# Output projection and first up chains computed in two parts of the tokens, with split weights kept, and the last conditioning columns moved into the up stage

## The chip, the cores and the metric
The kernel runs on one core of one Trainium2 chip. The metric is the device time of one execution in microseconds. Three executions took 1133.63, 1133.76 and 1136.33 us; their median is 1133.76 us. TensorE does the matrix products (PE in the profile), ScalarE (ACT), VectorE (DVE) and GpSimd (POOL) the rest, and SyncE (SP) issues the DMA copies.

## The reference
One inference step of one decoder layer, for a prompt of 512 tokens and 8 samples of one token each, model width 1024. The samples have their own conditioning vectors. What matters here is the part behind the mixing stage:

```python
mix = (jax.nn.sigmoid(z_pool) * y_pool + jax.nn.sigmoid(z_att) * y_att) @ w_out   # 1024 x 1024
x = x + gate_m * rms_norm(mix, g_post_mix)
h = modulate(rms_norm(x, g_pre_ffn), shift_f, scale_f)
hu_ext = jnp.concatenate([conv_hist, h @ w_up], axis=1)                            # 1024 x 5632
hc = b_conv
for j in range(CONV_W):                                                            # width 3, causal
    hc = hc + hu_ext[:, j:j + T] * w_conv[j]
a, b = jnp.split(hc, 2, axis=-1)
ffn = (jax.nn.gelu(a, approximate=True) * b) @ w_down                              # 2816 x 1024
x = x + gate_f * rms_norm(ffn, g_post_ffn)
```

The vectors shift, scale and gate come from silu(c) @ w_ada + b_ada, six times 1024 columns. The prompt and the samples go through the same weights. The updated key and value caches of the samples are outputs as well: almost all of their rows are copies of the inputs, shifted by one.

## The kernel before, in words
Activations lie transposed: channels on the 128 partitions, the 520 tokens (512 of the prompt and 8 samples) along the free dimension, eight tiles of 128 channels. All large products are made in three terms, high part of weights by high part of activations, high by low, low by high, each with fp32r operands. A unit is a block of weights, 128 output channels by 1024 input channels (512 KB). For each of the eight tiles of a unit and each of the three terms, TensorE issues two products, one for each half of 260 tokens (`blocks`, L1289): 48 products a unit. The sums go to two accumulators in turn, `acc[0]` and `acc[1]`; the engine that evacuates one counts `acc_free` up, and `take` waits for it.

A unit is loaded by SP into one of four raw buffers (`unit`, L333), which waits until the unit four before has been split (`lo_ready`). ACT writes the high part (`split`, L651), DVE the low part (L892). There are two places for split weights; a place is reused when TensorE is done with the unit in it (`unit_done`). The split of unit n + 2 stands behind unit n in ACT's and DVE's order. Every engine works its own list of instructions in order, SP too; the lists are written out by hand and meet at semaphores.

The units in order are 60 of the combined projection, 14 of the mixing stage, 8 of the output projection (`out`), 44 of the up projection (22 pairs (i, 0) and (i, 1), the a and the b half), and 24 of the down projection.

Output projection: for each of its units ACT copies the sum to `mixT` (L817) and writes its square to `sq` (L820), DVE adds that to `ssq` (L1212). Two more pieces lie between these units on TensorE. The conditioning vectors are made from w_ada in 24 steps of 256 columns: SP loads 1 MB (`ada_load`, L345), TensorE multiplies it (`ada`, L1333, 16 instructions), DVE evacuates, TensorE folds the parts (`fold`, L1343), DVE adds the bias (`modulation`). The last four steps (`OADA` to `OADA + 3`) give gate_f, which only the last norm uses. They have two buffers, `ada_last`; the load of step s waits until step s - 2 has been multiplied. TensorE issues them behind output units 4 to 7. In SP's list two of the loads come behind the load of output unit 3 and two behind that of unit 7. The old convolution inputs of the samples are transposed before the output projection (L1640), while TensorE waits for the merged activations.

Then the two norms, all tokens at once. Post norm: sum over partitions (`sum_columns`, L1355), reciprocal root on ACT and DVE (`inverse_root`, `root`), spread over the partitions (`spread`, L1361), and for each of eight tiles two DVE operations that update x (L1231, L1233). ACT squares the new x (L826), POOL adds the eight squares one after another (`sum_tiles`, L590), and sum, root and spread come again. Then DVE multiplies (L1250), ACT modulates (L680) and writes the high part (L683), DVE the low part (L964); the first up unit takes its tiles as they come.

Up chain i, two units: ACT evacuates a sum twice, into `he` (L842) and, times the last tap plus the bias, into `cv` (L843). DVE adds the two other taps, ACT takes the Gelu of the a half, DVE multiplies, ACT writes the high and DVE the low part of the result.

Beside each up unit SP issues one pair of cache copies (`copy`, L356); three pairs of such copies lie between output loads 0 to 2 and three between 3 to 5.

Of the kernel before, what the change touches and what calls it, by code (L numbers as in the profile page):

```python
# [12 lines left out]
P = 128  # L13
# [55 lines left out]

SUMS = (  # L70
    [("pair", p, k) for p in range(PAIRS) for k in range(NU)] + [("map", i) for i in range(8)] + [("pp", i) for i in range(8)]
    + [("pa", i) for i in range(8)] + [("out", i) for i in range(8)] + [("up", i, h) for i in range(FT) for h in range(2)]
# [6 lines left out]
PLACE = [0, 1, 2] + [n % 2 for n in range(1, len(UNITS) - 2)]  # L79
LAST = {n: max(i for i in range(n) if PLACE[i] == PLACE[n]) for n in range(3, len(UNITS))}  # L80
# [10 lines left out]
def program(nc, ins, outs):  # L91
# [5 lines left out]
    with ExitStack() as ctx:  # L97
# [42 lines left out]
        norm_u = put("norm_u", [KT, TC], F32, r_z)  # L140
# [19 lines left out]
        ada_raw += [put(f"ada_last{i}", [KT, 2 * P], F32, r_z + FULL + AW * i) for i in range(2)]  # L160

        def ada_slot(s):
            return ada_raw[s if s < SADA else 2 if s == SADA else 8 + s % 2 if s < OADA else 10 + s % 2]
# [3 lines left out]
        w_lo.append(put("w_lo2", [UW], F32R, r_more + UW * 4))  # L167
        S = new("S", [2, 2, 256])
# [51 lines left out]
        g_hi, g_lo = put("g_hi", [FT, TC], F32R, r_ff), put("g_lo", [FT, TC], F32R, r_ff + FT * TC * 4)  # L220
        r_cv = r_ff + 2 * FT * TC * 4
        cv = [[put(f"cv{a}{b}", [TC], F32, r_cv + (2 * a + b) * 2080) for b in range(2)] for a in range(2)]
        gm = [put(f"gm{b}", [TC], F32, r_cv + (4 + b) * 2080) for b in range(2)]
# [6 lines left out]
        conv_rows = put("conv_rows", [2 * NB, P], F32, r_ada)  # L230
        cst = put("cst", [2, NB * 2 * FT], F32, r_ada + 8192)
# [13 lines left out]
        psR = acc[1][:, 0, 400:405]  # L245
        accv = [a[:, :, 0:HALF] for a in acc]
        roots = {1: psT, 2: psS, 3: psS, 4: psS}

        def rs_p(n):
            return roots[n][:, 0:TP]  # L250

        def rs_s(n):
            return roots[n][:, TP:TP + NB] if n == 1 else roots[n][:, TP + P - NB:TP + P]

        def halves(x):
            return x.rearrange("p (a b) -> p a b", a=2)

# [50 lines left out]
        conv_used, conv_turned, ssqd = sem("conv_used"), sem("conv_turned"), sem("ssqd")  # L308
# [11 lines left out]
        def steps_to(t):  # L320

            return t // STEPS * (STEPS + 2) + t % STEPS

# [4 lines left out]
        def _(sp):  # L328
# [178 lines left out]
            sp.wait_ge(pv_done, 1)  # L507
            sp.dma_start(conv_rows[0:2 * FT, :, :], ins["state_conv"][0].rearrange("b j (m c) -> m (b j) c", c=P)).then_inc(conv_loaded, 16)
# [12 lines left out]
            ada_load(OADA + 3)  # L521

            for i in range(FT):
                for h in range(2):
                    unit(("up", i, h), block_of(w_up, i * P + h * FF))
                    copy(2, 2 * i + h + 36)

# [29 lines left out]
        def _(pool):  # L557
# [25 lines left out]
            def sum_tiles(base, first):  # L583
                for k in range(KT):
                    pool.wait_ge(squared, first + k + 1)
                    if k == 0:
                        pool.tensor_copy(ssq[:, :], sq[:, 0, :]).then_inc(ssqd, 1)
                    else:
                        pool.wait_ge(ssqd, base + k)
                        pool.tensor_tensor(ssq[:, :], ssq[:, :], sq[:, k % 2, :], ALU.add).then_inc(ssqd, 1)  # L590
# [41 lines left out]
            sum_tiles(8, 0)  # L632

            pool.wait_ge(tail_stored, 32)
            for i in range(FT):
                for half in range(2):
                    evacuated(pool, ("up", i, half))
# [1098 lines left out]
```

## Time and profile before
| | |
|---|---|
| median of three executions | 1133.76 us |
| the profiled execution | 1135.69 us, of which the span of the trace is 1133.8 us |
| TensorE products | busy 1059.3 us, 93% of the span |
| VectorE, ScalarE, GpSimd | busy 485.5, 417.8 and 119.7 us |
| mean granted TensorE clock | 0.955 of full speed |
| data moved by DMA | 216.01 MB, mean 191 GB/s |

The times of a trace are microseconds from the start of the span. Busy time of TensorE counts a product from issue to its modelled end, so that a busy row does not say that it works at its peak; the distance between starts says that. The span is 1.9 us shorter than the execution around it.

### The profile page before, as it was taken

The page shows a single profiled execution, that of the slowest core. Times are in us where ns is not written, and L with a number is a line of the kernel's source. Part 1 is how long each engine was busy: PE and PEld are TensorE (multiplying, and loading weights), DVE is VectorE, ACT ScalarE, POOL GpSimd, SP SyncE. Part 2 cuts the span into 40 slices and gives each one's busy share as a digit, 9 for nine tenths or more (in the row PEclk, how much of TensorE's full clock was granted, in tenths as well). Part 3 has the DMA queues.
Part 4 walks back from the last instruction along what each step waited for, and adds up shares of the span by engine and source line. Part 5 has one row for each costly group of instructions (what it writes and reads, how often), then busy time and mean ns, then how long its engine had stood idle before and what let it go on. Part 6 is the DMA issues. An engine that isn't in the chain of part 4 may idle for free.

```text
span 1133.8 us, 20595 instructions
## 1 busy us (share of the span) xinstructions
PE 1059.3 (93%) x8653; PEld 991.8 (87%) x8653; DVE 485.5 (43%) x884; ACT 417.8 (37%) x667; POOL 119.7 (11%) x165
## 2 busy tenths in 40 slices
PE   5999999999999999979898795599999999999996
PEld 3899999999999999868748794599999999999994
DVE  5533233322432244254814335656565655522224
ACT  5424423332443234244202233544444544422222
POOL 1000300040004001405402202200000000000000
PEclk8899999999999999979999897699999999999996
DMA  9885767567656774243926537066666666555312
GB/s 324 247 277 199 224 223 250 186 216 244 236 186 212 244 243 131 77 139 120 309 98 199 184 111 252 27 198 225 223 224 222 219 220 210 156 172 162 117 36 75
DMA packets 226856, 216.01 MB, mean 191 GB/s; under 512 B 6173, under 2 KB 191901, under 8 KB 226749
## 3 DMA queue, kind: packets, MB, share of 16 engines
q1 hardware_dynamic: 226765, 214.70, 58.2%
q8 instruction: 69, 1.13, 0.5%
q14 instruction: 22, 0.18, 0.0%
HBM read 207.27 MB, written 96.03 MB: 268 GB/s over the span
## 4 chain that ended last, share of the span: by engine, by line
PE 87%; DVE 5%; ACT 2%; POOL 2%; issue 1%; SPq 1%; DMA 1%; ACTq 0%; POOLq 0%; DVEq 0%
PE acc L1289 74%; PE psT L1581 2%; PE psS L1453 2%; PE psT L1467 2%; PE psS L1333 2%; POOL tha L630 1%; POOL ssq L590 1%; PE psS L1441 1%; PE psS L1343 1%; DMA ada_first<-in_w_ada 1%; PE psT L1481 1%; PE psS L1439 1%; PE psS L1557 1%; DVE xT L1233 1%; ACT norm_u L680 1%
## 5 line engine op out<-in xcount | busy, mean ns | idle before, releaser
L1289 PE MATMUL acc<-act_hi,w_hi 128*128 128x260 f32 x1824 | 379.3, 289 | 20.4 <-DVE act_lo L1138 7.2
L1289 PE MATMUL acc<-act_hi,w_lo 128*128 128x260 f32 x1824 | 371.0, 285 | 0.0
L1289 PE MATMUL acc<-act_lo,w_hi 128*128 128x260 f32 x1824 | 370.7, 285 | 0.0
L892 DVE TENSOR_TENSOR w_lo<-raw,w_hi 128x1024 fp32r<-128x1024 f32 x150 | 191.7, 1279 | 374.7 <-ACT w_hi L651 374.1
L1289 PEld LDWEIGHTS acc<-act_hi,w_hi 128*128 128x128 f32 x1824 | 284.9, 191 | 29.3 <-issue 23.9
L1289 PEld LDWEIGHTS acc<-act_lo,w_hi 128*128 128x128 f32 x1824 | 285.3, 191 | 0.0
L1289 PEld LDWEIGHTS acc<-act_hi,w_lo 128*128 128x128 f32 x1824 | 284.9, 191 | 0.0
L651 ACT ACTIVATE w_hi<-raw 128x1024 fp32r<-128x1024 f32 x150 | 157.0, 1046 | 203.7 <-PE acc L1289 193.7
L1289 PE MATMUL acc<-g_hi,w_hi 128*128 128x260 f32 x352 | 71.0, 283 | 0.0
L1289 PE MATMUL acc<-g_hi,w_lo 128*128 128x260 f32 x352 | 70.8, 282 | 0.0
L1289 PE MATMUL acc<-g_lo,w_hi 128*128 128x260 f32 x352 | 70.6, 282 | 0.0
L842 ACT ACTIVATE he<-acc 128x520 f32<-128x520 f32 x44 | 26.7, 607 | 86.8 <-PE acc L1289 86.8
L1289 PEld LDWEIGHTS acc<-g_lo,w_hi 128*128 128x128 f32 x352 | 54.3, 188 | 0.0
L1289 PEld LDWEIGHTS acc<-g_hi,w_hi 128*128 128x128 f32 x352 | 54.2, 188 | 0.0
L1289 PEld LDWEIGHTS acc<-g_hi,w_lo 128*128 128x128 f32 x352 | 54.2, 188 | 0.0
L707 ACT ACTIVATE S<-S,stat 128x256 f32<-128x256 f32 (+1 forms) x64 | 31.2, 489 | 41.7 <-DVE stat L1016 41.7
L1264 DVE TENSOR_TENSOR cv<-cv,hsc 128x8 f32<-128x8 f32 x44 | 7.6, 174 | 88.9 <-ACT cv L843 88.9
L597 POOL COPY u_tail<-uT 128x46 f32<-128x46 f32 x4 | 0.9, 224 | 404.4 <-ACT uT L733 404.4
L730 ACT ACTIVATE qkvT<-acc 128x520 f32<-128x520 f32 x16 | 17.4, 1088 | 56.2 <-PE acc L1289 56.2
L638 POOL COPY hu_tail<-he 128x10 f32<-128x10 f32 x44 | 9.1, 207 | 259.8 <-ACT cv L843 259.8
L843 ACT ACTIVATE cv<-acc,vec 128x520 f32<-128x520 f32 x44 | 34.3, 781 | 0.0
L624 POOL TENSOR_TENSOR cached<-cached,qB 128x2048 f32<-128x2048 f32 x6 | 27.6, 4593 | 60.3 <-ACT qB L779 60.3
(248 smaller groups left out, 1126.9 us busy)
## 6 DMA issues: line engine op xcount, KB each, us to landing
out_k_sample<-in_cache_k_w SPq DMA_DIRECT2D x89, 368.0 KB
out_v_sample<-in_cache_v_w SPq DMA_DIRECT2D x89, 368.0 KB
raw<-in_w_in SPq DMA_DIRECT2D x60, 512.0 KB, 6.1
raw<-in_w_up SPq DMA_DIRECT2D x44, 512.0 KB, 5.8
ada_mid<-in_w_ada SPq DMA_DIRECT2D x11, 1024.0 KB, 9.8
ada_first<-in_w_ada SPq DMA_DIRECT2D x9, 1024.0 KB, 9.4
raw<-in_w_down SPq DMA_DIRECT2D x16, 512.0 KB, 4.1
out_k_sample<-in_cache_k_w SPq DMA_DIRECT2D x16, 511.0 KB
```

Source lines behind the costliest of these rows:

```text
L624: pool.tensor_tensor(kS[i][:, :, :], kS[i][:, :, :], qB[i % 2][:, :, :], ALU.mult).then_inc(prod_done, 1)
L651: act.activation(w_hi[PLACE[n]][:, 0:unit_cols(n)], raw[:, n % RAW, 0:unit_cols(n)], ACT.Copy).then_inc(hi_ready, 1)
L707: act.activation(S[:, t % 2, h, lo:], S[:, t % 2, h, lo:], ACT.Exp, bias=stat[:, j // 4, 0, h, j % 4:j % 4 + 1], scale=-1.0, accum_out=sta ...
L730: act.activation(by_class(qkvT[:, k, :]), in_time(of(s)), ACT.Copy, scale=scale).then_inc(free(s), 1)
L842: act.activation(halves(he[half][m][:, 2:2 + TC]), of(s), ACT.Copy)
L843: act.activation(halves(cv[half][m][:, :]), of(s), ACT.Identity, bias=bc, scale=w2).then_inc(free(s), 1)
L892: dve.tensor_tensor(w_lo[PLACE[n]][:, 0:cols], raw[:, n % RAW, 0:cols], w_hi[PLACE[n]][:, 0:cols].bitcast(F32), ALU.subtract).then_inc(lo_ ...
L1289: ins_ = pe.matmul(acc[b][:, half, 0:HALF], w, x[:, t, half * HALF:(half + 1) * HALF], start=first and i == 0 and j == 0, stop=last and i ...
L1333: ins_ = pe.matmul(out[32 * (k % 4):32 * (k % 4) + 32, :], siluT[:, MC * k:MC * k + 32], ada_slot(s)[:, k, :], start=k < 4, stop=k >= 4)
L1453: ins_ = pe.matmul(psO[64 * h:64 * h + 64, :], v, PT[:, t % 2, (2 * h + c) * P:(2 * h + c + 1) * P], start=c == (1 if i == 0 else 0), stop ...
L1467: ins_ = pe.transpose(blk(psT[:, 0:512], 2 * h + c), blk(S[:, (t - 1) % 2, h, :], c), ident[:, :])
L1581: ins_ = pe.matmul(psT[0:NB * NS, 512:1024], prT[:, g, at:at + NB * NS], vS[i][:, j, :], start=i == 0 and j == 0, stop=i == 5 and j == 3)
```

## The change
Tokens 0 to 255 are part 0, tokens 256 to 519 part 1 (`PARTS`); part 2 means all. The eight output sums are made for part 0 and then for part 1, and so are the first three up chains (`EARLY = 3`); chains 3 to 21 go over all tokens as before. A sum of one part takes 24 products, of 256 or 264 columns. Each output unit's split weights get a place of their own (places 3 to 10, in memory that the mixing stage has left), so that part 1 uses them again; up chains 1 and 2 use places 3 to 6 in the same way, and chain 0 the two old ones. The norms run by parts as well: `sum_columns` and `spread` over two and three columns of tokens (roots 2 and 3 for part 0, 4 and 5 for part 1, 6 for the last norm). Part 0's post norm, squares and second root stand between the output sums of part 1. In the first output pair and the first up pair, two sums are taken side by side, tile by tile as the activations come. The gate's columns (`OADA` and on) are multiplied and folded behind up chains 8 to 15; they have one buffer, and SP's loads stand behind the raw loads of chains 6, 8, 10 and 12. The six pairs of cache copies of the output stage go behind the first six up loads. The transposes of the old convolution inputs come behind output sum 4. Cut to its core:

```diff
+PARTS = ((0, 256), (256, TC), (0, TC))
+EARLY = 3
+CHAINS = [(i, part) for part in range(2) for i in range(EARLY)] + [(i, 2) for i in range(EARLY, FT)]
 @@ SP
             for m in range(8):
                 unit(("out", m, 0), block_of(w_out, m * P))
-                if m < 3:
-                    copy(1, m)
-                if 3 <= m < 6:
-                    copy(2, m - 3)
-                if m == 3:
-                    sp.wait_ge(merged_split, 8)
-                    ada_load(OADA)
-                    ada_load(OADA + 1)
-            ada_load(OADA + 2)
-            ada_load(OADA + 3)
+                if m == 4:
+                    sp.wait_ge(merged, 8)
+                    sp.dma_start(conv_rows[...], ...).then_inc(conv_loaded, 16)
             for i in range(FT):
                 for h in range(2):
                     unit(("up", i, h), block_of(w_up, i * P + h * FF))
                     copy(2, 2 * i + h + 36)
+                    if i < EARLY:
+                        copy(*((1, 2 * i + h) if 2 * i + h < 3 else (2, 2 * i + h - 3)))
+                if i >= 6 and i % 2 == 0 and i < 14:
+                    if i == 6:
+                        sp.wait_ge(half_done, 8)
+                    else:
+                        sp.wait_ge(ada_done, OADA + (i - 6) // 2)
+                    sp.dma_start(ada_slot(OADA)[:, :, :], ...)
 @@ ACT
+            for m in range(8):
+                act.wait_ge(half_done, m + 1)
+                out_evac(m, 1)
+                if m < 2 * EARLY - 2:
+                    split(N["up", 0, 0] + 2 + m)
+                if m == 0:
+                    root(2)
+                if m in (1, 2, 3):
+                    for k in range(3 * m - 3, min(3 * m, KT)):
+                        square(0, k)
+                if m == 5:
+                    root(3)
+                if m == 6:
+                    modulate(norm_u, a_f, 24, KT, 4, 0, 0)
+                    modulate(norm_u, a_f, 24, KT, 4, 1, 0)
...
+            root(4)
+            up_evac(0)
+            up_evac(1)
+            for k in range(3):
+                square(1, k)
+            up_evac(2)
+            for k in range(3, 6):
+                square(1, k)
+            up_evac(3)
+            square(1, 6)
+            square(1, 7)
+            up_evac(4)
+            root(5)
+            up_evac(5)
             for k in range(KT):
-                modulate(norm_u, a_f, 24, KT, 5, k)
+                modulate(norm_u, a_f, 24, 2 * KT, 5, k, 1)
             act.activation(seed[:, 13:14], eps[:, :], ACT.Gelu_apprx_tanh)
+            gelu(0)
+            gelu(1)
 @@ DVE
+            for m in range(8):
+                add_square(("out", m, 1), 8, m, 1)
+                if m < 2 * EARLY - 2:
+                    split(N["up", 0, 0] + 2 + m)
+                if m == 0:
+                    inverse_root(2)
+                if m in (1, 2, 3):
+                    for k in range(3 * m - 3, min(3 * m, KT)):
+                        post(mixT, gg_m, 2, k)
+                if m == 5:
+                    inverse_root(3)
...
 @@ TensorE
+            def part_blocks(s, slot, part, tiles_, hi, lo, last=True):
+                c, out = tokens(part), acc_of(s, part)
+                for t in tiles_:
+                    wh, wl = blk(w_hi[slot], t), blk(w_lo[slot], t)
+                    for j, (w, x) in enumerate(((wh, hi), (wh, lo), (wl, hi))):
+                        ins_ = pe.matmul(out, w, x[:, t, c], start=t == 0 and j == 0, stop=t == KT - 1 and j == 2)
+                return ins_
...
             for m in range(8):
-                slot = ready(("out", m, 0))
-                take(("out", m))
+                take(("out", m, 1))
+                part_blocks(("out", m, 1), PLACE[N["out", m, 0]], 1, range(KT), act_hi, act_lo).then_inc(half_done, 1)
                 if m == 0:
-                    pe.wait_ge(merged_split, 8)
-                blocks(("out", m), slot, [(i, i) for i in range(KT)], act_hi, act_lo).then_inc(unit_done, 1)
-                if m >= 4:
-                    ada(OADA + m - 4)
-                if m >= 5:
-                    fold(OADA + m - 5)
+                    pe.wait_ge(conv_used, 2)
+                    pe.wait_ge(ssqd, 8)
+                    sum_columns(2)
+                if m == 1:
+                    spread(2)
+                if m == 5:
+                    pe.wait_ge(ssqp, 8)
+                    sum_columns(3)
+                if m == 6:
+                    spread(3)
...
-            for i in range(FT):
+            for i in range(EARLY, FT):
                 for half in range(2):
...
+                if 8 <= i < 16:
+                    s = OADA + (i - 8) // 2
+                    if i % 2 == 0:
+                        ada(s)
                     else:
-                        ins_ = blocks(s, slot, [(k, k) for k in range(KT)], act_hi, act_lo)
-                    ins_.then_inc(unit_done, 1)
+                        fold(s)
```

## Rows read from the trace of the kernel before
**Rows 1.** The page's 40 slices, TensorE's busy tenths.
```profile
PE   5999999999999999979898795599999999999996
```
**Rows 2.** The chain that ended last, 636 to 760 us: start, us, what.
```profile
636.85 31.72 PE acc L1289 x240
...
668.57 1.00 PE psS L1333 x16
...
676.51 0.54 PE psS L1343 x4
...
714.78 2.31 PE acc L1355 x10
...
733.09 26.94 PE acc L1289 x222
```
**Rows 3.** Timeline of ACT in the up stage: start, us, instruction, [idle before <-releaser].
```profile
826.37 0.61 ACT L842 ACTIVATE he<-acc 128x520 f32<-128x520 f32 x1 [0.41 <-PE acc L1289]
...
832.14 0.61 ACT L842 ACTIVATE he<-acc 128x520 f32<-128x520 f32 x1 [3.54 <-PE acc L1289]
```
**Rows 4.** Groups by line, several stretches: xcount | busy us, mean ns | idle before.
```profile
L817 ACT ACTIVATE mixT<-acc 128x520 f32<-128x520 f32 x8 | 4.7, 587 | 0.0
...
L672 ACT ACTIVATE vec<-acc 128x264 f32<-128x264 f32 x1 | 0.4, 391 | 0.2 <-PE acc L1380 0.2
...
L680 ACT ACTIVATE norm_u<-norm_u,mod,a_f 128x512 f32<-128x512 f32 x8 | 6.4, 802 | 3.7 <-DVE norm_u L1250 3.7
...
L830 ACT ACT_TABLE_LOAD x1 | 1.3, 1283 | 0.0
...
L1231 DVE SCALAR_TENSOR_TENSOR mixT<-mixT,gg_m,psS 128x512 f32<-128x512 f32 x8 | 5.9, 736 | 0.0
...
L590 POOL TENSOR_TENSOR ssq<-ssq,sq 128x520 f32<-128x520 f32 x7 | 10.8, 1542 | 1.1 <-ACT sq L826 0.3
...
L1361 PE MATMUL psS<-ident,nrm 128*128 128x128 f32 x10 | 2.6, 426 | 2.9 <-DVE nrm L960 2.9
...
L1640 PE MATMUL psT<-ident,conv_rows 44*128 44x44 f32 x16 | 1.2, 234 | 0.0
```
**Rows 5.** One stretch of the up stage: busy us of each engine, PEclk, DMA share, GB/s.
```profile
800.00:850.00 50.00, 50.00 (x419) 50.00 (x418) 29.95 (x44) 23.99 (x36) 1.66 (x8) 1.00 0.67 225
```
**Rows 6.** The same for single microseconds, and TensorE's restart at 509.61 in its timeline.
```profile
641.00:642.00 1.00, 1.00 (x7) 1.00 (x7) 0.00 (x0) 0.00 (x0) 0.00 (x0) 0.50 1.08 383
...
509.61 0.69 PE L1289 MATMUL acc<-act_hi,w_hi 128*128 128x260 f32 x2 [2.41 <-DVE mixed_lo L1146]
...
510.00:511.00 1.00, 1.00 (x7) 1.00 (x7) 0.13 (x1) 0.00 (x0) 1.00 (x1) 0.50 0.00 0
...
513.00:514.00 1.00, 1.00 (x10) 1.00 (x10) 0.76 (x1) 0.20 (x1) 0.00 (x0) 0.94 0.00 0
...
716.00:717.00 1.00, 1.00 (x6) 0.99 (x5) 0.00 (x0) 0.00 (x0) 0.00 (x0) 0.50 0.00 0
...
731.00:732.00 1.00, 0.61 (x5) 0.41 (x4) 0.66 (x1) 0.97 (x2) 0.00 (x0) 1.00 0.00 0
```
**Rows 7.** SP: issues of ada_last, two raw issues of its timeline, and its waits.
```profile
L345 SPq DMA_DIRECT2D ada_last<-in_w_ada x4: 367/368/582, 636.7 to 676.6; - x4
...
676.98 1.46 SPq L333 DMA_DIRECT2D raw<-in_w_up  x1
...
807.40 0.37 SPq L333 DMA_DIRECT2D raw<-in_w_up  x1
...
SPq L345 <- PE psS L1333: 22.1, 2, 15.5
```
**Rows 8.** Weight splits behind that load; the page's row of raw issues, us to landing.
```profile
684.94 1.06 ACT L651 ACTIVATE w_hi<-raw 128x1024 fp32r<-128x1024 f32 x1 [7.27 <-DMA raw<-in_w_up]
...
686.04 1.23 DVE L892 TENSOR_TENSOR w_lo<-raw,w_hi 128x1024 fp32r<-128x1024 f32 x1 [7.07 <-ACT w_hi L651]
...
raw<-in_w_up SPq DMA_DIRECT2D x44, 512.0 KB, 5.8
```

More of the change, by code:

```diff
@@ L75 @@
 SUM = {s: i for i, s in enumerate(SUMS)}
-PLACE = [0, 1, 2] + [n % 2 for n in range(1, len(UNITS) - 2)]
-LAST = {n: max(i for i in range(n) if PLACE[i] == PLACE[n]) for n in range(3, len(UNITS))}
+PLACE = {0: 0, 1: 1, 2: 2}
+for n in range(3, len(UNITS)):
+    what, i, h = UNITS[n]
+    if what == "out":
+        PLACE[n] = 3 + i
+    elif what == "up" and 1 <= i < EARLY:
+        PLACE[n] = 3 + 2 * (i - 1) + h
+    else:
+        PLACE[n] = 1 - PLACE[max(m for m in PLACE if PLACE[m] < 2)]
+LAST = {n: max(m for m in range(n) if PLACE[m] == PLACE[n]) for n in PLACE if any(PLACE[m] == PLACE[n] for m in range(n))}
 def tiles(x):
@@ L167, in program @@
         w_lo.append(put("w_lo2", [UW], F32R, r_more + UW * 4))
+        WB = UW * 4
+        kept = [(at, at + WB) for at in (r_att, r_att + 2 * WB, r_o, r_o + 2 * WB, r_ada, r_ada + 2 * WB)]
+        kept += [(r_more + i * WB, r_s + 3 * TC * 4 + i * WB) for i in range(2)]
+        for i, (hi_at, lo_at) in enumerate(kept):
+            w_hi.append(put(f"w_hi{3 + i}", [UW], F32R, hi_at))
+            w_lo.append(put(f"w_lo{3 + i}", [UW], F32R, lo_at))
         S = new("S", [2, 2, 256])
@@ new lines, in _ @@
+            act.activation(seed[:, 13:14], eps[:, :], ACT.Gelu_apprx_tanh)
+            gelu(0)
+            gelu(1)
+            for j in range(2 * EARLY, len(JOBS)):
+                up_evac(j)
+                i, half, part = JOBS[j]
+                u = N["up", i, half]
+                if u + 2 >= N["up", EARLY, 0]:
+                    if part == 2:
+                        split(u + 2)
+                if part == 1 and i == 0:
+                    split(N["up", EARLY, half])
+                if j == 2 * EARLY + 1:
+                    gelu(2)
+                if j % 2:
+                    gelu(j // 2)
@@ new lines, in _ @@
+            norm_samples(5)
+            for k in range(KT + 2):
+                if k < KT:
+                    normed(5, k)
+                if k >= 2:
+                    lo_of(norm_u, k - 2, 28, 1)
+            up_taps(4)
+            up_taps(5)
+            gate(0)
+            gate(1)
+            mark(dve.memset(ssq[:, :], 0.0))
+            mine()
+            for j in range(2 * EARLY, len(JOBS)):
+                i, half, part = JOBS[j]
+                up_taps(j)
+                if part == 2:
+                    split(N["up", i, half] + 2)
+                if part == 1 and i == 0:
+                    split(N["up", EARLY, half])
+                if j == 2 * EARLY + 1:
+                    gate(2)
+                if j % 2:
+                    gate(j // 2)
+                if part == 2 and half and 8 <= i < 16:
+                    s = OADA + (i - 8) // 2
+                    if i % 2 == 0:
+                        ada_evac(s)
+                    else:
+                        modulation(s)
```

428 lines of the change are left out of this document (266 added, 162 removed).

## The prediction
> **What bounds the kernel now.** The first view is the page's 40 slices of 28.3 us [rows 1]: TensorE's digit is 9 nearly everywhere; it falls at both ends, a little around the middle, and to 5 only in slices 25 and 26 (680 to 737 us). So time is won only where TensorE stands still, and lost wherever something new makes it stand still. The second view, the chain of waits [rows 2], says where it stands still now. Output projection: five units in 31.72 us, then three with ada products between them, to 690.3. Then DVE, ACT and POOL work: two inverse roots, each behind a sum over columns, and eight serial POOL additions, until the last tile of up unit 0 starts at 733.1. In these 43 us TensorE has little to do. Third, the ACT rows of the up stage [rows 3]: evacuations start at 826.37 (unit (8,0)) and 832.14 (unit (8,1)), one unit every 5.77 us, with TensorE full [rows 5]: 48 products of 260 columns at 0.120 us. Every microsecond by which a unit's weights come late is there paid in full.
>
> **Part 1, what the split saves.** I start at 636.7, when the merged activations are split; nothing before it changes but the order in which TensorE takes tiles. Up unit 6 (the first not split by tokens) starts now at 734.0 + 5 x 5.766 = 762.8, which is 126.1 us after. Half a unit is 24 products: 24 x 0.1201 = 2.88 us (256 and 264 columns instead of 260 twice, so the sum stays).
> Half durations are bounded from rows [rows 4]: never under half the whole operation, never over it; ACT's 264 columns out of PSUM took 0.39 beside 0.59 for 520, so I take two thirds for ACT, and little over half for DVE (0.41 for 0.74, 0.38 for 0.69) and POOL (0.8 for 1.55).
> Output, first tokens: two sums side by side tile by tile leave 0.9 us after 636.7; weights of the third unit are split only then (1.06 ACT, 1.23 DVE, rows 8), so it starts at 3.3. Six halves 17.3, the clock's loss as today 2.9 (below), sixteen conv transposes now in TensorE's full path 1.2: 24.7.
> Output, last tokens: eight halves 23.0, two column sums and two spreads over two of five columns each 2.5 (today 2.31 and 1.3 for all five). Waits: 0.7 for the root; then ACT must take its squares of the new x behind DVE's posts (three at 0.85 to 1.0, behind a 1.23 weight split), and only then evacuates, so sums 5 and 6 wait 3.2 and 2.5. With the last root that is 32.4.
> Up, first tokens: two chains side by side paced by ACT's modulation (0.80 a tile and a high part behind it; 0.82 taken for both at half), 6.9; sum columns and the wait for the first evacuation (three ACT operations) 2.7; two halves and a spread 6.5; wait 2.8 because ACT's squares stand before the evacuation; half 2.8; wait 3.1 for POOL's last addition; sum, half and spread 5.0: 29.8. Up, last tokens: wait 2.4, eight tiles at 0.82 6.6, then 4.0 for the Gelu table (1.28), two Gelus and two gates that stand ahead of the evacuation, four halves 11.5 and one wait 1.6: 26.1.
> Sum 24.7 + 32.4 + 29.8 + 26.1 = 113.0 against 126.1: saved 13.1. If none of these waits came the saving would be 13.1 + 26 = 39; if each half cost as much as a whole, none. I take 13.1, since each wait is an in-order queue read off the code with a row for each operation.
> The kept weights need no second split and no second load: that is a saving of nothing, as DMA and DVE have room, and its cover is the 5.77 us a unit in which DVE works 3.5 [rows 3, 4]. The copies put three units later ride in a DMA stage at 0.67 share [rows 5]. Both at 0; were the DMA full, the 4.5 MB of six late pairs would cost up to 20 us at the 225 GB/s of that row.
>
> **Part 2, the clock in the split stretch.** A granted clock of 0.50 is 1.2 GHz, 1.00 is 2.4. After a 7 us wait that ended at 636.85 TensorE ran at 0.50 until past 642: five units took 31.72 instead of 28.83, 2.9 lost. After a 2.4 us wait (to 509.6) it ran at 0.50 for 3 us, losing 1.4 [rows 2, 6]. My list has six waits of 2.4 us or more; some losses fall on a chain that another engine paces. Nothing to 6 x 2.9 = 17; I take three of 1.4: 4.2 lost.
> The Trainium skill, "TensorE: Matmul & The Clock Gate", section "HAM oscillation — how this bites in real kernels", says that work cut into short bursts between waits starts each burst on the slow clock again. By that rule all of the stretch would pay, as in rival 2 below.
>
> **Part 3, ada products in the up stage.** Four ada products (1.00 each) and four folds (0.54) stood in the output stage, inside my 126.1; now they stand behind up pairs 8 to 15, where TensorE is full: +6.2 [rows 2]. DVE's small evacuations there hide in its room (29.95 of 50 us busy, rows 5).
>
> **Part 4, the loads of these columns.** This is what decides. The queue of SP is in order. Before, two buffers; now one, so load s+1 waits until ada product s is done. SP reaches that wait right behind the raw load of up(8,1), and TensorE issues the product only behind up(8,1) itself. The raw loads of the weights of up(9,0) and later are queued behind the wait. Today up(9,0) is loaded at 807.4 [rows 7], four buffers ahead; up(8,1) ends at 832.1 [rows 3]. In the changed kernel, in the same frame, its load goes out when up(8,1) and the ada product have ended, 833.1, behind a load of 1 MB. All of the lead of 25 us is gone. The trace has this sequence once already, hidden by the norm: SP waited 15.5 us at L345, the product's last matmul ended at 676.5, ada_last was issued at 676.6, raw for w_up at 676.98, and ACT's hi split, which waited on that DMA, started at 684.94; DVE's lo split, 1.23 long, started at 686.04 [rows 7, 8]. From product to usable weights, with 0.1 for the handoff, 687.35 - 676.5 = 10.85 us, and in the up stage nothing covers it: TensorE has no other unit split. Then comes the slow clock, 2.9 as after the 7.2 us wait. It comes three times: at i = 8, 10 and 12 (the load at 6 waits for something long past). 3 x (10.85 + 2.9) = 41.3. Bounds: the landing cannot be under the 5.8 median of raw from w_up alone [rows 8], and no clock loss: 3 x 8.6 = 26; above, the next weights, queued behind two more copies, come late as well, by 2 us: 3 x 15.75 = 47.
> The Trainium skill, "DMA: Bandwidth & Descriptors", section "Two DMAs through the same engine are not ordered", says that within a queue descriptors start in order; so the weights' do stand behind the megabyte. The trace's 7.96 against 5.8 agrees; were they served side by side the sum would be 6.5 less.
>
> **The sum.** -13.1 + 4.2 + 6.2 + 41.3 = +38.6. The profiled execution took 1135.69 (span 1133.8 and 1.9 around it): 1174.3. The median of the runs, 1133.76, lies 1.9 under it; I predict 1172.
>
> **Rivals.** (1) The SP wait is harmless. Place: L345's successor behind up(8,1); price 41.3; it decides if the weights of up(9,0) are in before TensorE gets there, that is if SP came to its wait only after the product. For it: today SP loses 15.5 us in the like wait and only 7.3 of it reach ACT, none TensorE. Against: that had the norm behind it; here SP comes to its wait a unit before 807.4, 31 us ahead of the product, and only four raw buffers exist. Without it 1172 - 41.3 = 1131, within 0.3% or a little faster. (2) The slow clock holds in the whole split stretch: of its 672 products 250 would cost 0.1 us more, +25, less my 4.2: 1192. For it: the clock was 0.50 at 716 us, inside the norm; against: at 731 to 732, with TensorE busy 0.61 between short waits, it stood at 1.00 [rows 6]. (3) The waits of part 1 mostly don't come, since two PSUM sums and kept weights decouple more than I grant: 26 more saved, 1146. For it: DVE and ACT are 60% and 48% busy even in the up stage [rows 5]; against: each wait follows from one queue's order. (4) That the change doesn't do what it says: none seen; the halves fit the code.
>
> **How the numbers follow.** Forecast 0.78, rival 1 0.06, rival 2 0.09, rival 3 0.07. A measurement tells 0.3%, 3.4 us, from no change. Rival 1 falls half to "same", half to "faster", with a little more for both if rivals 1 and 3 come together: faster 0.04, same 0.03, slower 0.93. The range leaves out rival 1 and most of 3 and of 2: 1152 to 1188.
>
> **What would show it.** In the trace after: three idle stretches of TensorE of 10 to 11 us in the up stage, each behind an ada product, ended by DVE's w_lo, with ACT's w_hi waiting for the DMA of raw from w_up, and the clock at 0.50 behind each; SP waiting some 30 us three times on the ada product. Between 636.7 and up(3,0) 117 us. The forecast is wrong if these stretches are absent or under 5 us, or if the split stretch takes under 100 us.

## The result, and the profile after

The changed kernel takes 1195.68 us (median of 4 runs, 1193.3 to 1196.74) against 1134.01 of the kernel before on the same chip: ratio 1.0535 with a 95% interval of [1.0519, 1.0550], +61.7 us. Of all executions below two fell in a slow state, one of the kernel before (2047 us) and one of the last experiment (1315 us), and no ratio uses them. The forecast was 1172, range 1152 to 1188: slower, as said, but by 23 us more. The profiled execution took 1196.74, its span is 1194.9, the mean granted clock 0.939 (before: 1135.69, 1133.8 and 0.955).

The page's slices first: TensorE's busy tenths and the share of the DMA engines, each slice 29.9 us now.
```profile
PE   5999999999999999798987767799779699999996
DMA  9875777577757752438314663045344777655412
```
Before, TensorE's deep hollow was the two 5s at slices 25 and 26 [rows 1]. Now a shallower and longer one stands at slices 22 to 26 (627 to 777 us: 7, 7, 6, 7, 7), and behind it, where every slice was a 9, come 7, 7 and 6 (slices 29, 30 and 32, in the up stage).

The hollows have two causes. The chain of waits of the changed kernel, 853 to 933 us (start, us, what), shows the second one:
```profile
853.49 1.04 PE psS L1550 x16
854.97 6.08 DMA raw<-in_w_up
861.07 1.06 ACT w_hi L727
862.16 1.24 DVE w_lo L1034
863.44 13.66 PE acc L1497 x96
...
889.05 1.04 PE psS L1550 x16
890.52 6.12 DMA raw<-in_w_up
896.66 1.06 ACT w_hi L727
897.75 1.24 DVE w_lo L1034
899.03 14.54 PE acc L1497 x96
...
925.51 1.04 PE psS L1550 x16
926.99 6.11 DMA raw<-in_w_up
```
Product of ada columns, load, two splits, and then TensorE again: three times. SP's waits and its timeline around the first, then TensorE's restart:
```profile
SPq L598 <- PE psS L1550: 65.7, 3, 29.7
```
```profile
854.55 0.37 SPq L598 DMA_DIRECT2D ada_last<-in_w_ada  x1
854.97 0.58 SPq L406 DMA_DIRECT2D raw<-in_w_up  x1
```
```profile
863.44 0.80 PE L1497 MATMUL acc<-act_hi,w_hi 128*128 128x260 f32 x2 [8.95 <-DVE w_lo L1034]
```
SP's first wait lasts 29.7 us; the other two are shorter, 17.5 and 18.6. The weights go out 0.42 us behind the ada load that SP waited for. The other two restarts stand at 899.03 and 935.50, 8.98 idle each. The clock behind the first (as [rows 5]: busy of each engine, granted clock, DMA share, GB/s):
```profile
866.00:867.00 1.00, 1.00 (x6) 1.00 (x6) 0.00 (x0) 0.88 (x1) 0.00 (x0) 0.50 1.07 377
...
868.00:869.00 1.00, 1.00 (x10) 1.00 (x10) 1.00 (x2) 0.00 (x0) 0.00 (x0) 1.00 0.78 202
```
It is 0.50 until 867 and 1.00 from 868. From 863.44 to the next ada product at 889.0 pass 25.6 us where four units and a fold need 4 x 5.766 + 0.54 = 23.6: 2.0 us lost to it. Counted alike the next two restarts lose 2.9 (899.03 to 925.51) and 1.8 (935.50 to 960.89).

The first cause is in the split stretch. From the last split of the merged activations (636.5) to the start of up(3,0) (784.3) pass 147.8 us; before it was 126.1, forecast 117.2. The chain of waits there:
```profile
655.84 5.40 SPq L429
...
664.92 0.67 SPq L406
665.63 6.52 SPq L429
...
675.62 1.27 SPq L406
676.94 7.16 SPq L429
...
696.17 10.58 DMA raw<-in_w_up
706.78 1.07 ACT w_hi L727
```
L429 issues the copies, L406 the weights, L727 is ACT's split: the chain runs through SP's queue from 651 to 696. ACT's timeline says who waited:
```profile
678.44 1.06 ACT L727 ACTIVATE w_hi<-raw 128x1024 fp32r<-128x1024 f32 x1 [9.25 <-DMA raw<-in_w_up]
...
680.97 0.37 ACT L893 ACTIVATE mixT<-acc 128x264 f32<-128x264 f32 x1
...
689.23 1.06 ACT L727 ACTIVATE w_hi<-raw 128x1024 fp32r<-128x1024 f32 x1 [7.61 <-DMA raw<-in_w_up]
...
692.43 0.42 ACT L903 ACTIVATE sq<-xT 128x256 f32<-128x256 f32 x1 [2.14 <-DVE xT L1374]
...
694.46 0.37 ACT L893 ACTIVATE mixT<-acc 128x264 f32<-128x264 f32 x1
...
697.99 1.06 ACT L727 ACTIVATE w_hi<-raw 128x1024 fp32r<-128x1024 f32 x1 [2.88 <-DMA raw<-in_w_up]
```
Four splits of up weights, up(1,0) to up(2,1), stand in ACT's queue between the evacuations of output units (L893, L896), and the root and squares behind them. Each waits for its load, and holds back an evacuation that needs no up weight. TensorE waits for the accumulator:
```profile
695.16 0.59 PE L1507 MATMUL acc<-act_hi,w_hi 128*128 128x264 f32 x1 [4.84 <-ACT sq L896]
...
703.94 0.59 PE L1507 MATMUL acc<-act_hi,w_hi 128*128 128x264 f32 x1 [3.25 <-ACT sq L896]
```
The page's row of raw issues from w_up (count, KB, us to landing) moved from 5.8 [rows 8] to
```profile
raw<-in_w_up SPq DMA_DIRECT2D x44, 512.0 KB, 9.3
```
So +61.7 is made of 21.7 here (147.8 - 126.1), 6.2 of moved products, and three waits of 8.97 in the up stage with some 2.2 of slow clock behind each, 33.6: together 61.5.

### The profile page after: what moved, and what is told of

The parts are those of the page before. It is cut to its first block, busy times and chain, and to the rows that moved or that the text cites. A ratio compares the mean times of both kernels' runs of the same rounds, so it can differ in the third digit from the quotient of the medians.

```text
span 1194.9 us, 20788 instructions
## 1 busy us (share of the span) xinstructions
PE 1079.6 (90%) x8653; PEld 1010.9 (85%) x8653; DVE 497.8 (42%) x952; ACT 428.4 (36%) x739; POOL 120.9 (10%) x173
## 4 chain that ended last, share of the span: by engine, by line
PE 79%; DVE 7%; SPq 5%; DMA 3%; ACT 3%; issue 2%; POOL 1%; ACTq 0%; POOLq 0%
PE acc L1497 63%; PE acc L1507 3%; SPq L429 3%; DMA raw<-in_w_up 2%; PE psT L1800 2%; PE psS L1672 2%; PE psT L1686 1%; PE psS L1550 1%; DVE w_lo L1034 1%; POOL tha L703 1%; DMA ada_first<-in_w_ada 1%; PE psS L1660 1%; SPq L406 1%; PE psT L1700 1%; DVE xT L1374 1%
## 5 line engine op out<-in xcount | busy, mean ns | idle before, releaser
L1497 PE MATMUL acc<-act_hi,w_hi 128*128 128x260 f32 x1600 | 334.0, 290 | 35.2 <-DVE w_lo L1034 26.9
L1497 PE MATMUL acc<-act_hi,w_lo 128*128 128x260 f32 x1600 | 325.6, 285 | 0.0
L1497 PE MATMUL acc<-act_lo,w_hi 128*128 128x260 f32 x1600 | 325.6, 285 | 0.0
L727 ACT ACTIVATE w_hi<-raw 128x1024 fp32r<-128x1024 f32 x150 | 157.0, 1047 | 252.2 <-PE acc L1497 160.7
L1497 PE MATMUL acc<-g,w_hi 128*128 128x260 f32 x704 | 113.0, 283 | 0.0
L1507 PE MATMUL acc<-act_hi,w_hi 128*128 128x256 f32 (+1 forms) x224 | 75.9, 339 | 28.4 <-ACT sq L896 9.3
L1497 PEld LDWEIGHTS acc<-g,w_hi 128*128 128x128 f32 x704 | 96.4, 188 | 0.0
L1507 PE MATMUL acc<-act_lo,w_hi 128*128 128x256 f32 (+1 forms) x224 | 72.9, 326 | 0.0
L1507 PE MATMUL acc<-act_hi,w_lo 128*128 128x256 f32 (+1 forms) x224 | 72.5, 324 | 0.0
L1497 PE MATMUL acc<-g,w_lo 128*128 128x260 f32 x352 | 70.8, 282 | 0.0
L1497 PEld LDWEIGHTS acc<-g,w_lo 128*128 128x128 f32 x352 | 54.3, 188 | 0.0
```

Of the source, the lines that this page charges most:

```text
L727: act.activation(w_hi[PLACE[n]][:, 0:unit_cols(n)], raw[:, n % RAW, 0:unit_cols(n)], ACT.Copy).then_inc(hi_ready, 1)
L1497: ins_ = pe.matmul(acc[b][:, half, 0:HALF], w, x[:, t, half * HALF:(half + 1) * HALF], start=first and i == 0 and j == 0, stop=last and i ...
L1507: ins_ = pe.matmul(out, w, x[:, t, c], start=t == 0 and j == 0, stop=t == KT - 1 and j == 2)
```

## The experiments

Each one's ratio is against the kernel before, measured beside it on the same chip; a ratio in this text is followed by its 95% interval. Where the time of one changed kernel is taken from that of another, the two are medians from different chips in part, and the difference of the ratios can be 1 to 2 us away from it. Two questions came first: are these the two causes, and do they add up?

**Copies out of the way.** The changed kernel, with the six copy pairs taken from behind up(0) to up(2) and put into the down stage.
```
 SP, up stage
-                    if i < EARLY:
-                        copy(*((1, 2 * i + h) if 2 * i + h < 3 else (2, 2 * i + h - 3)))
 SP, down stage
+                    e = (3 * m + part) // 2
+                    if (3 * m + part) % 2 == 0 and e < 6:
+                        copy(*((1, e) if e < 3 else (2, e - 3)))
```


> The changed kernel with the six moved pairs of cache copies taken from behind the first six up loads and put behind down loads that have none. Theory A (the early up weights come late because each stands in SP's queue behind two pairs of copies, about 2 to 2.3 MB a unit at 230 GB/s): the waits of ACT's hi split for raw from w_up between 660 and 710 us (9.25, 7.61, 2.9 and 2.9) go, up unit (3,0) starts some 26 us earlier (758 instead of 784), time 1170. Theory B (they come late because of the ring of four raw buffers, or because a load waits for a split that the new order makes late): nothing moves, 1196.


Measured 1167.85 (1166.73 to 1171.89), ratio 1.0295 [1.0265, 1.0324]: 27.8 us back. From the last split to up(3,0) pass 120.8 us instead of 147.8, and from there to the end 410.5 against 410.6, so the copies cost nothing in the down stage. Theory A holds.

**Ada loads spaced.** The changed kernel, with the four ada loads behind up units 6, 11, 14, 17 and the products behind 8, 11, 14, 17, so that SP comes to each wait when the product before is long done.
```
-                if i >= 6 and i % 2 == 0 and i < 14:
+                if i in (6, 11, 14, 17):
 TensorE
-                if 8 <= i < 16:
-                    s = OADA + (i - 8) // 2
-                    if i % 2 == 0:
+                if 8 <= i < 20:
+                    s = OADA + (i - 8) // 3
+                    if (i - 8) % 3 == 0:
                         ada(s)
```


> The changed kernel with the last four ada loads placed behind raw loads of chains 6, 11, 14 and 17 and their products behind chains 8, 11, 14 and 17, so that SP comes to each wait when the product before is done or nearly so. Theory A (SP's in-order wait on the ada product costs 8.95 us three times, plus 2 to 3 us of slow clock each): the three idle stretches at 854, 890 and 926 us go, 34 us less, time 1162. Rival (the megabyte load itself delays the weights behind it, wherever it stands): idle stretches of 3 us or more stay behind each ada load, time above 1180.


Measured 1161.36 (1158.94 to 1165.93), ratio 1.0234 [1.0202, 1.0266]: 34.3 back, and no idle stretch of 9 us in the up stage is left. Theory A holds.

**Both.**


> Both edits of e1 and e2 on the changed kernel. Theory A: the two costs lie in different stretches and add, 26 + 34 = 60 us less than the changed kernel, time 1136, within 0.5% of the kernel before. Rival (the split order itself is slow, as the clock is low in it and ACT's order holds the accumulators): above 1150.


Measured 1136.34 (1130.75 to 1138.09, 10 runs), ratio 1.0004 [0.9986, 1.0022]. The two undone one by one gave 27.8 and 34.3, together 59.3: they nearly add up. What remains of the change brings nothing on balance: 120.4 us to up(3,0), 5.7 under before, and the 6.2 of the moved products eat that.

**The ada part on the kernel before**, first as in the change, then spaced.
```
-        ada_raw += [put(f"ada_last{i}", [KT, 2 * P], F32, r_z + FULL + AW * i) for i in range(2)]
+        ada_raw.append(put("ada_last", [KT, 2 * P], F32, r_more + 10240 + 3 * TC * 4))
 SP: the four loads of the output stage go, and in the up stage
+                if i >= 6 and i % 2 == 0 and i < 14:
+                    if i > 6:
+                        sp.wait_ge(ada_done, OADA + (i - 6) // 2)
```


> The kernel before with this one part of the change alone: the last four ada steps in one buffer, loads behind up chains 6, 8, 10, 12, products and folds behind chains 8 to 15. Output and up stay unsplit, copies stay in the output stage. Theory A: three idle stretches of 9 us as in the changed kernel and slow clock behind each; +34 for these and +6 for products in a full stage, less some 6 in the output stage, which no longer has them: 1168 to 1175. Rival (the stretches come only with the split order): 1134 to 1140.


Measured 1167.92 (1166.58 to 1169.62), ratio 1.0288 [1.0268, 1.0308], at the lower edge of theory A. The same three waits stand in a kernel without any split by tokens (TensorE's timeline; the third restart is at 906.96, 8.79 idle):
```profile
834.76 0.80 PE L1288 MATMUL acc<-act_hi,w_hi 128*128 128x260 f32 x2 [8.97 <-DVE w_lo L890]
...
870.68 0.80 PE L1288 MATMUL acc<-act_hi,w_hi 128*128 128x260 f32 x2 [9.16 <-DVE w_lo L890]
```


> The kernel before with the last four ada steps moved into the up stage as in e4, but with loads behind chains 6, 11, 14, 17 and products behind 8, 11, 14, 17. Theory A (moving the products costs their 6.2 us in the full up stage and gives back the same in the output stage; all the loss of e4 is SP's wait): within 0.3% of the kernel before, 1134. Rival (ada loads beside up weights and copies slow the up stage by traffic alone): 1140 or more.


Measured 1134.29 (1133.49 to 1135.75, 10 runs), ratio 1.0002 [0.9990, 1.0014]. Moving the products costs nothing on balance when the loads are spaced. This kernel also gives the measure for the split by tokens. It has none, keeps its six copy pairs in the output stage, and takes 120.2 us from the last split of the merged activations to up(3,0); the split kernel with both causes gone takes 120.4. So the 5.7 us under before are what the ada work leaves behind when it goes, and the split by tokens itself gained nothing in this stretch.

**The copies part on the kernel before.** Only the six pairs move, from the output units to the first six up units.
```
-                if m < 3:
-                    copy(1, m)
-                if 3 <= m < 6:
-                    copy(2, m - 3)
 up stage
+                    if i < 3:
+                        copy(*((1, 2 * i + h) if 2 * i + h < 3 else (2, 2 * i + h - 3)))
```


> The kernel before, with one edit: the six copy pairs that stood behind the first six output units stand behind the first six up units, as in the changed kernel; nothing else moves. Theory A (queue position and bytes): each unit of the early up weights then carries 2.2 MB ahead of it at some 235 GB/s, about 10 us a unit, as in the changed kernel; but here the up stage starts only after the second norm, at 734 us, and the weights of up(0) to up(2) are due 20 to 40 us later than the split kernel wants them. So the delay is covered here in large part: 1136 to 1145, and not the 28 that the same move costs in the split kernel. Rival B: the copies cost their 28 us wherever the output stage is short of them, since the DMA is the bound: 1160 or more. If A, the two edits of the change hurt each other: the copies are harmless alone and the split needs the weights early.


Measured 1138.87 (1137.06 to 1140.28), ratio 1.0039 [1.0024, 1.0055]: +4.5, not +28. The same move of the same bytes costs six times as much beside the split. ACT's waits in this kernel:
```profile
681.44 1.06 ACT L649 ACTIVATE w_hi<-raw 128x1024 fp32r<-128x1024 f32 x1 [5.65 <-DMA raw<-in_w_up]
...
692.08 1.06 ACT L649 ACTIVATE w_hi<-raw 128x1024 fp32r<-128x1024 f32 x1 [8.60 <-DMA raw<-in_w_up]
```
Two waits of 14.2 us in all, near the end of the output units. The two norms, in which TensorE has little to do, come right behind and cover most of it: from the last split to up(3,0) pass 130.3 us instead of 126.1.

**Is it the bytes, or the queue in which the split waits?** The kernel with spaced ada loads (1161), copies left where the change puts them; only the four splits of up(1,0) to up(2,1) stand later in ACT's and DVE's queues.
```
 ACT and DVE, output sums of the last tokens
-                if m < 2 * EARLY - 2:
-                    split(N["up", 0, 0] + 2 + m)
+                if m in (4, 7):
+                    split(N["up", 0, 0] + 2 + m // 7)
 ACT, modulation of the first tokens (DVE alike)
+                if k in (5, 7):
+                    split(N["up", 0, 0] + 4 + k // 7)
```


> The changed kernel with spaced ada loads (1161 in an earlier run), with its six copy pairs left behind the first six up units; the weight splits of up(1,0) to up(2,1), which ACT and DVE run behind the last tokens' output sums 0 to 3, stand later in both queues: two behind sums 4 and 7, two in and behind the modulation. No load and no copy moves. Theory A (the late weights cost through the in-order queues of ACT and DVE: a split that waits for its DMA holds back the evacuation, squares and updates that need no up weight, while up(1,0) itself is wanted only some 25 us later): most of the 25 to 28 us comes back without touching the DMA, 1138 to 1148, and ACT's wait for raw from w_up falls from 21 us in this stretch to a few. Rival B (the weights themselves are too late for TensorE): the wait moves to up(1,0) to up(2,1) and stays, 1155 to 1161.


Measured 1141.02 (1139.15 to 1142.42), ratio 1.0057 [1.0043, 1.0070]: 20.3 of the 25 us between 1161.36 and 1136.34 come back with no load or copy moved. The seventh up load goes out 52.1 us behind the first here and 53.4 in the changed kernel, so the loads are as late as before. ACT's wait for these loads, in the kernel with spaced ada loads and in this one (us in total, times, longest):
```profile
ACT w_hi L728 <- DMA raw<-in_w_up: 21.6, 4, 8.2
```
```profile
ACT w_hi L728 <- DMA raw<-in_w_up: 1.4, 1, 1.4
```
The DMA carried about as much: 227 GB/s from 650 to 720 us against 231 in the kernel with spaced ada loads. Late loads were the occasion; most of the price was the place of the waiting split ahead of work that didn't need it. Some 5 us stay with the moved copies, as in the kernel before (+4.5).

**Copies in the up stage, where there is a lead.** The kernel with both causes gone (1136), its six pairs behind up units 7, 9, ... 17.
```
+                    if h and 7 <= i < 19 and i % 2:
+                        e = (i - 7) // 2
+                        copy(*((1, e) if e < 3 else (2, e - 3)))
```


> The kernel with both moves undone or spaced (1136 in an earlier run), but its six copy pairs stand one each behind the second halves of up units 7, 9, 11, 13, 15 and 17, instead of in the down stage. The up stage moves 0.5 MB of weights and 0.74 MB of copies each 5.77 us, 225 to 238 GB/s; with one more pair of 1 MB every 23 us (every fourth unit) the need is 270 GB/s. Theory A (only the position ahead of the early up weights costs): four weight buffers and a lead of 25 us absorb 4.3 us of extra traffic every fourth unit: 1134 to 1138. Rival B (the up stage is already at the DMA's limit of about 235 GB/s): the lead shrinks by 3 to 4 us with each pair, 25 us by the sixth, and with the ada loads waits of w_hi on the raw load begin: 1142 to 1160.


Measured 1142.86 (1138.93 to 1146.39), ratio 1.0077 [1.0055, 1.0099]: +6.5 over the kernel it is made from (8 by the ratios), at the low end of rival B. Where its lead has run out, the window of 900 to 940 us, first in the kernel it is made from and then in this one, and two of ACT's waits in it:
```profile
900.00:940.00 40.00, 40.00 (x343) 39.28 (x342) 22.66 (x37) 19.09 (x27) 1.45 (x7) 1.00 0.73 242
```
```profile
900.00:940.00 40.00, 35.17 (x299) 34.22 (x298) 20.56 (x32) 16.89 (x24) 1.24 (x6) 1.00 0.71 247
```
```profile
908.87 1.06 ACT L729 ACTIVATE w_hi<-raw 128x1024 fp32r<-128x1024 f32 x1 [4.01 <-DMA raw<-in_w_up]
...
936.50 1.06 ACT L729 ACTIVATE w_hi<-raw 128x1024 fp32r<-128x1024 f32 x1 [6.40 <-DMA raw<-in_w_up]
```
While ACT waits for loads, the engines move 247 GB/s at a share of 0.71. Without the extra pairs nobody waits, TensorE is busy all 40 us, and the engines move 242 GB/s at 0.73: the share doesn't tell the stage that keeps up from the one that doesn't. The up stage needs 222 GB/s even without ada loads (0.52 MB of weights and 0.75 MB of copies each 5.77 us), so it had little room. With the pairs TensorE is busy 35.2 of these 40 us.

**Can the split be made to pay?** Four orders, each on the kernel with both causes gone. First the output stage: the split of output unit 1 ahead of the last two merges, and two updates and squares of x behind each of sums 1 to 4 instead of three, three, two behind 1 to 3.
```
-                if m in (1, 2, 3):
-                    for k in range(3 * m - 3, min(3 * m, KT)):
+                if m in (1, 2, 3, 4):
+                    for k in (2 * m - 2, 2 * m - 1):
 and for ("pa", 3), ACT and DVE: split(N[u] + 2) ahead of the merge instead of behind it
```


> Kernel e3 (copies and ada loads out of the way) with two changes of order in the output stage: the weights of output unit 1 are split ahead of the last two merges, so that the two side-by-side sums can start when the tiles come, and posts and squares go two to a sum over sums 1 to 4 instead of three, three and two over 1 to 3. Theory A (in e3 TensorE waits 5.7 us for that split, and 3.8 us for ACT's squares that stand ahead of an evacuation): 4.4 + 3 us less than e3, time about 1129. Rival (both waits are hidden behind the norm's chain of posts, squares and POOL additions): as e3, 1136.


Measured 1143.07 (1140.37 to 1143.55), ratio 1.0074 [1.0053, 1.0095]: both expectations missed. Slower than its base by 6.7. With the second of the two edits alone:


> The kernel with both moves undone or spaced (1136), with only one of the two edits that together made it 7 us slower: the updates of x and their squares stand two behind each of the last tokens' sums 1 to 4, instead of three, three and two behind 1 to 3. Theory A (the POOL chain of additions ends one sum later, and everything behind the third column sum with it): 1141 to 1144, with TensorE waiting 5 to 6 us on ssq before the column sum. Rival B (the weight split ahead of the merges cost the 7): 1135 to 1137.


Measured 1141.71 (1136.57 to 1144.07), ratio 1.0064 [1.0041, 1.0087], +5.4: the updates' order makes most of it, and the time lies where theory A had it. POOL's chain of additions ends later, and the column sum waits for it, 4.3 us instead of 0.66 in its base (5 to 6 were expected):
```profile
690.05 1.01 PE L1575 MATMUL psT<-ones,ssq 128*128 128x1 f32 x4 [4.32 <-POOL ssq L665]
```
In all TensorE waits 3 us more in this stretch than in its base; the rest is slow clock behind the waits, some 4 us by the estimate under Part 2 below. The split's order is left with 1.4 us, which these intervals don't tell from none; it gained nothing, since the first pair then waited for the accumulator of the last sum before it: `[6.79 <-DVE tha L1344]` at 632.98, in place of `[5.71 <-DVE w_lo L1036]` at 630.14 in its base.

Second, the up stage: evacuations ahead of squares, the fifth column sum behind all six first sums, Gelus and gates ahead of the last tokens' modulation.
```
 ACT
             up_evac(1)
-            for k in range(3):
-                square(1, k)
             up_evac(2)
...
+            root(5)
             act.activation(seed[:, 13:14], eps[:, :], ACT.Gelu_apprx_tanh)
             gelu(0)
             gelu(1)
+            for k in range(KT):
+                modulate(norm_u, a_f, 24, 2 * KT, 5, k, 1)
```


> Kernel e3 with another order in the first up chains: ACT evacuates the third to sixth sum earlier among its squares, the column sum of part 1 stands behind all six first sums on TensorE, and the first two Gelus and gates stand ahead of part 1's modulation instead of behind it. Theory A (TensorE's 8.5 us of waits for cv and 2.5 for POOL come from the order of these queues): 8 to 11 us less than e3, time about 1127. Rival (DVE's eight posts at 0.85 us pace this stretch whatever the order): at most 3 us less, 1133 or more.


Measured 1133.96 (1130.27 to 1136.61, 10 runs), ratio 0.9994 [0.9980, 1.0008]: 2.4 us under its base by the medians, 1 by the ratios, which the intervals don't tell from none; the rival's "at most 3 us less" holds. The three waits for ACT's cv fall from 8.5 us to 3.3 and come back as two others of TensorE's waits (us in total, times, longest):
```profile
PE psS L1575 <- POOL ssq L665: 5.8, 1, 5.8
...
PE acc L1509 <- DVE act_lo L1110: 5.4, 1, 5.4
```
Both order edits together:


> Kernel e3 with the edits of e5 and e6. Theory A: they add, 15 to 18 us less than e3, time about 1119, faster than the kernel before by over 1%. Rival (the slow clock fills what the waits leave): 1127 or more.


Measured 1142.35 (1140.38 to 1142.69), ratio 1.0066 [1.0048, 1.0084]: the edits don't add up to a gain. The rival's number holds, but that the slow clock fills what the waits leave was not tested. No kernel tried here is measurably faster than the one before.

## Why the prediction failed

The microseconds from the last split of the merged activations to the start of up(3,0), worked out alike from each trace (end of the last act_lo of the merge; evacuation of up(3,0) less 5.8): before 126.1, changed 147.8, copies down 120.8, ada loads spaced 145.1, both undone 120.4, splits later 124.3; on the kernel before, ada spaced 120.2, copies moved 130.3. By these:

**The failed step: "The copies put three units later ride in a DMA stage at 0.67 share [rows 5]. Both at 0".** It cost 27.8 us. Three errors are in it. The row was that of 800 to 850 us, but the copies go out from 651 to 704. The share of 0.67 was read as a third of room, and it isn't: SP issues a unit's weights every 5.2 us where one copy pair goes with them (658.0 to 689.2, both undone), and every 9.9 us with two (664.9 to 704.4, changed). The mean share in these stretches is 0.73 and 0.62, the rate 248 and 221 GB/s, so that the stretch with the later loads shows the lower share. A pair adds 4.7 us, and the seventh up load goes out 53.4 us behind the first instead of 26.8, 26.6 more for six pairs. My bound, "up to 20 us", had the bytes, 0.75 MB a pair, but a rate of 225 GB/s where 0.75 MB in 4.7 us is 160. And I asked only if the DMA had room, not who would wait: the split kernel wants its up weights split among the output sums, in the very stretch that received the copies, and the queues of ACT and DVE pass the lateness on to work that needs no up weight. With the four splits later in these queues and the loads as late, 20.3 us come back; on the kernel before, the same move costs 4.5.

**Part 1 and its clock: forecast -13.1 + 4.2 = -8.9, measured -5.7** with the copies away. All of the 5.7 comes without any split too (120.2 us in the kernel before with spaced ada loads): the 126.1 held ada work that left the stretch, and the forecast counted that as a gain of the split. Of the four blocks of the forecast, with the 4.2 of clock apart, output for the first tokens took 27.7 instead of 24.7 (632.58 to 660.23, both undone), for the last 32.3 instead of 32.4, up for the first 32.1 instead of 29.8, for the last 28.3 instead of 26.1: 7.4 more, of which the 4.2 were forecast.

Missed in the first block: the first pair of output units, taken side by side, needs the second unit's weights too, and their split stands behind the last merge; in the changed kernel the pair ended 5.5 us behind the starting point, not 0.9, and the third unit started 7.8 behind it, not 3.3 (644.28, idle 2.11 until w_lo). Part of these 4.5 us is slow clock, which the forecast had as 2.9 of its own. ACT's modulation took 0.95 a tile, not 0.82 (16 tiles, 2.1 us in all); its first operation alone took 0.59 for half the tokens where the whole takes 0.80 [rows 4], near three quarters. The waits that the forecast named one by one came to 17.5 instead of 20.3. Behind the output sums 2.6 came for the 3.2 and 2.5, and the last 1.6 did not come; 1.2 and 0.7 came that were not on the list; the others lay within 0.7 of their forecasts (3.4 for 2.8 and 3.7 for 4.0 behind ACT's evacuations). In kind this part was right: each wait comes from one queue's order.

**Part 2.** The slow clock was not separated from the rest by a run, but the traces allow an estimate: for each microsecond of the stretch, TensorE's busy time by what the granted clock lacks to 1. For the three restarts above this gives 2.1, 3.1 and 1.9, near the 2.0, 2.9 and 1.8 counted there. In the stretch it gives 8.7 us before and 13.4 with both undone: 4.7 more, and 4.2 was forecast. In the changed kernel it gives 24.4, and TensorE idles 37.9 us instead of 21.0. So of the 27 us that the copies add here, some 17 are waits and some 11 are slow clock behind the waits. The rival by which the clock stays slow in the whole stretch is out: the granted clock from 650 to 720 us is 0.78 in the changed kernel and 0.93 with both undone. That its price, 25, is near 24.4 is luck; the waits that made it were those of the copies.

**Part 3, +6.2** stands: from up(3,0) to the end pass 376.9 us with both undone and 370.9 before, 6.0 more. The spaced kernel made of before shows the other side: the products left a stretch that paid for them too, and the move nets 0.

**Part 4: mechanism right, size 34 instead of 41.3.** Three idle stretches behind an ada product, ended by w_lo, with the clock at 0.50 behind each; undoing it gave 34.3, doing it alone cost 32.8. SP's waits were 29.7, 17.5 and 18.6, not three times 30, and the idle stretches 9 us, not 10 to 11. The term that was off is "from product to usable weights ... 10.85": measured 8.95, since the load took 6.1 us from its issue, not 7.96. Here the engines moved 332 to 364 GB/s from 856 to 862 us, and SP's issue of the load took 0.58 us against 1.46 in the precedent [rows 7]; why the precedent was slower no run tells. The megabyte of ada columns landed 5.0 to 5.2 us from its issue, the weights behind it, half as many bytes, 1.3 to 1.5 us later, each of the three times; in the precedent 6.1 us and 2.2 later. The Trainium skill, "DMA: Bandwidth & Descriptors", section "Two DMAs through the same engine are not ordered", says that within a queue descriptors start in order, and these landings agree. The clock took 1.8 to 2.9 instead of 2.9.

So the sum missed by 28 for the copies, -7 for part 4 and 3 for part 1: the 24 between 1172 and 1195.7. Rival 1 (a harmless wait) is refuted, rival 3 (the waits of part 1 don't come) too. The range failed because a term set to 0 with a bound of its own, 20 us, was not let into it.

## What to carry to other kernels

A wait is paid by what stands behind it in the same queue: when loads are moved, look in every engine's queue for the instruction that waits for them and ask what independent work it stands ahead of; moving that instruction gave back 20 us without moving a byte. When a load has to wait for a consumer, put it where that wait is over before the loads behind it are due: three waits that used up the whole lead cost 34 us, spaced ones nothing. Before crediting a reordering with a gain, measure the same stretch in a kernel from which the same work was moved and nothing reordered; here that took the whole gain away. And read the DMA's room from the stretch that receives the traffic, by the cadence of the issues, not from a share.

## What the runs showed of the hardware

A mean DMA share of 0.6 to 0.7 was no sign of room in this mix: with copies from cache to output among the loads the DMA engines moved 219 to 247 GB/s at 0.63 to 0.71 while ACT waited for loads, and 242 at 0.73 where nobody waited. What sets these rates no run tells. With a megabyte and a weight load at the head of an emptied queue they moved 332 to 364 GB/s at shares of 1.01 to 1.10 (856 to 862 us, changed). The full queue also shows at the issuer: a copy's issue takes 0.7 us when the queue is free, and the first copy behind each of five early up loads took 5 to 7 (7.16 at 676.94).

Waits of TensorE were dearer than their length. In the changed stretch some 17 us of added waits came with some 11 us of slow clock by the estimate above, and each 9 us wait in the up stage with 1.8 to 2.9.
